# Further rows' parts in one operand, the 128 rows stored first, a later broadcast, and the last gate product in parts

## The reference, cut to what matters

```python
def hierarchical_moe(n, ...):              # 16 experts, 2 for each token
    for e in range(N_EXPERTS):
        hdn = jax.nn.silu(t @ w1[e]) * (t @ w3[e])
        out = out + gate[:, e:e + 1] * (hdn @ w2[e])

    h = h + hierarchical_moe(rms_norm(h, W['g_ffn'][l]), ...)
    gate = jax.nn.sigmoid(rms_norm(h, W['g_ple'][l]) @ W['w_ple_gate'][l])
    h = h + gate * (p[l] @ W['w_ple_proj'][l])
return rms_norm(h, W['g_final'])
```

## Time and profile before

| | |
|---|---|
| median of 3 runs | 770.13 us (769.03 to 772.84) |
| profiled execution | 769.56 us, of which the span of its instructions is 767.9 us |
| PE busy | 730.7 us, 95% |
| DVE, ACT, POOL busy | 396.6 us (52%), 318.6 us (41%), 135.2 us (18%) |
| mean granted clock of TensorE | 0.982 |
| DMA | 169.10 MB, mean 220 GB/s |

### The profile page before, as it was taken

How to read it: one execution, slowest core, us unless ns; L and a number is a source line. 1 busy time by engine, 2 the same in 40 slices (tenths; PEclk the granted TensorE clock), 3 DMA queues, 4 the chain that set the end, 5 groups by cost and what they waited for, 6 DMA issues and landing times.

```text
span 767.9 us, 11872 instructions
## 1 busy us (share of the span) xinstructions
PE 730.7 (95%) x4428; PEld 627.7 (82%) x4429; DVE 396.6 (52%) x623; ACT 318.6 (41%) x554; POOL 135.2 (18%) x168
## 2 busy tenths in 40 slices
PE   3999999999999989999999999999999999879995
PEld 2887778787888858989987987999999999738884
DVE  4987987894655466313431331343344333366663
ACT  5608659664402125314431331443444433384242
POOL 3645105060001002000000000000000000043320
PEclk9999999999999969999999999999999999999999
DMA  9909924404043258877997495699999999353202
GB/s 320 289 1 321 266 51 150 165 1 159 33 155 147 90 212 293 294 253 271 360 369 243 176 358 175 253 343 353 348 351 330 335 336 366 117 193 111 103 35 82
DMA packets 78127, 169.10 MB, mean 220 GB/s; under 512 B 7556, under 2 KB 19272, under 8 KB 78088
## 3 DMA queue, kind: packets, MB, share of 16 engines
q1 hardware_dynamic: 69968, 141.53, 52.5%
q0 software_dynamic: 4448, 14.62, 6.1%
q10 hardware_dynamic: 3672, 12.42, 4.2%
HBM read 144.50 MB, written 24.05 MB: 220 GB/s over the span
## 4 chain that ended last, share of the span: by engine, by line
PE 92%; DVE 2%; ACT 2%; DMA 1%; issue 1%; POOL 1%; ACTq 1%; POOLq 0%; DVEq 0%
PE bank L712 34%; PE bank L911 32%; PE bank L920 5%; PE bank L701 5%; PE bank L922 5%; PE bank L921 5%; PE bank L693 3%; PE bank L833 2%; PE bank L889 2%; DMA regT<-y_scratch,slots 1%; DMA y_scratch<-regN 1%; ACT ring_r L415 0%; ACTq L1087 0%; ACT regN L1067 0%; DVE regN L1337 0%
## 5 line engine op out<-in xcount | busy, mean ns | idle before, releaser
L712 PE MATMUL bank<-ring_r,regT_r 128*128 128x512 f32 x624 | 162.3, 394 | 1.7 <-DVE regT_r L1444 1.7
L712 PEld LDWEIGHTS bank<-ring_r,regT_r 128*128 128x128 f32 x624 | 116.5, 188 | 28.0 <-issue 4.5
L911 PE MATMUL bank<-regT,ring 128*128 128x128 f32 (+1 forms) x1024 | 125.4, 284 | 1.9 <-issue 0.9
L911 PEld LDWEIGHTS bank<-regT,ring 128*128 128x128 f32 x1024 | 123.3, 194 | 4.5 <-issue 4.1
L911 PE MATMUL bank<-regN,ring 128*128 128x128 f32 (+1 forms) x1024 | 123.2, 281 | 0.1
L911 PEld LDWEIGHTS bank<-regN,ring 128*128 128x128 f32 x1024 | 122.1, 191 | 1.3 <-issue 0.6
L617 POOL DMA_INDIRECT regT<-n_scratch,idsi x17 | 16.0, 940 | 323.5 <-PEq L878 209.4
L1653 DVE TENSOR_TENSOR regR<-regR,bank 128x320 f32<-128x320 f32 x32 | 15.6, 486 | 103.4 <-ACT regR L1198 103.4
L712 PE MATMUL bank<-regT_r,ring_r 128*128 128x256 f32 (+1 forms) x256 | 65.3, 344 | 2.9 <-DVE ring_r L423 2.9
L921 PE MATMUL bank<-ring_r,regR_r 128*128 128x512 f32 (+1 forms) x160 | 63.0, 394 | 0.0
L1198 ACT ACTIVATE regR<-bank 128x320 f32<-128x320 f32 x32 | 14.0, 437 | 109.5 <-PE bank L911 109.4
(11 more groups left out here) (283 smaller groups left out, 1206.5 us busy)
## 6 DMA issues: line engine op xcount, KB each, us to landing
ring<-in_w_exp_down SPq DMA_DIRECT2D x16, 2048.0 KB, 15.8
ring<-in_w_exp_gate SPq DMA_DIRECT2D x16, 2048.0 KB, 9.5
ring<-in_w_exp_up SPq DMA_DIRECT2D x16, 2048.0 KB, 16.2
ring<-in_w_in SPq DMA_DIRECT2D x4, 2048.0 KB, 10.7
y_scratch<-zeros SPq DMA_DIRECT2D x4, 1408.0 KB, 12.6
y_scratch<-regN ACTq DMA_DIRECT2D x11, 384.0 KB
h<-in_x_sample SPq DMA_DIRECT2D x8, 512.0 KB, 10.3
y_scratch<-zeros SPq DMA_DIRECT2D x4, 1024.0 KB, 11.2
```

The lines of the kernel that those rows point to most:

```text
L712: q = nc.tensor.matmul(out, a, b, start=(n == 0), stop=(n == len(passes) - 1))
L911: q = nc.tensor.matmul(bank[b][:, col:col + n], slot3(s)[:, k, f * P:(f + 1) * P], moe["xT", par][:, k, 0:n], start=(k == 0), stop=(k == K ...
```

## The change

Four edits.

1. The further rows' high and low parts lie side by side in one tile, `more_parts`, 64 columns wide. One matmul against the high weights gives both products (high by high in partitions 0 to 31 of the bank, low by high in 32 to 63); a second one, 32 columns wide, adds high by low. That is 8 matmuls for each half of the output where there were 12. The two parts of the bank must be added afterwards: DVE adds partitions 32 to 63 of bank 4 and of bank 5 to what was copied, and a new semaphore `y2_summed` tells of it. PE waits for it before it fills these banks again. `hid`'s product, its high copy and its low part are made separately for the 128 and for the further rows (two operations where one was). A clearing of 32 more partitions of bank 5 is added ahead of the first expert.
2. ACT stores the 128 rows before it copies the further rows, and stores those when `y2_summed` has come.
3. The broadcast into `gF` is issued after the first tile's high parts (after `high_n3T(0)`), no longer ahead of `take_embed(1, 0)`.
4. The last tile's gate product comes in parts of 512, 256 and 256 columns, each with its own sigmoid, multiply, add, multiplication by `gF` and sum of squares; the three sums are added on DVE, then DVE scales columns 0 to 511 and ACT columns 512 to 1023 by 1/rms, and SP stores the two halves.

The diff, cut to its core:

```diff
-            def down(out, par, lo, n, j, chunks):
+            def down(out, par, j, chunks):
...
+            def further_down(out, par, j):
+                for f in range(F4):
+                    q = nc.tensor.matmul(out[0:2 * CAP2, :], more_parts[:, f, :], down_hi[f][j], start=(f == 0), stop=(f == F4 - 1))
+                    if f < F4 - 1:
+                        for g in range(2 * f, min(2 * f + 2, F4)):
+                            nc.tensor.matmul(out[0:CAP2, :], more_hi[:, g, :], down_low(par, g, j), start=False, stop=False)
+                return q
...
                                 pe.wait_ge(ylo_drained, 2 * r)
+                                pe.wait_ge(y2_summed, r)
...
-                    down(bank[4], par, P, CAP2, 0, range(F4)).then_inc(tlo_full, 1)
-                    down(bank[5], par, P, CAP2, 1, range(F4)).then_inc(thi_full, 1)
+                    pe.wait_ge(more_done, 2 * r + 2)
+                    further_down(bank[4], par, 0).then_inc(tlo_full, 1)
+                    further_down(bank[5], par, 1).then_inc(thi_full, 1)
...
             pe.wait_ge(yhi_drained, 2 * (NE + more))
+            pe.wait_ge(y2_summed, NE + more)
...
             def hid_high_half(r, half):
+                two = slice(2 * half, 2 * half + 2)
                 act.wait_ge(hid_raw, 2 * r + half + 1)
-                nc.scalar.activation(hid_hi[:, 2 * half:2 * half + 2, :], hid[:, 2 * half:2 * half + 2, :], ACT.Copy).then_inc(hid_high, 1)
+                nc.scalar.activation(hid_hi[:, two, :], hid[:, two, :], ACT.Copy).then_inc(hid_high, 1)
+                act.wait_ge(more_raw, 2 * r + half + 1)
+                nc.scalar.activation(more_hi[:, two, :], more_hid[:, two, :], ACT.Copy).then_inc(more_high, 1)
...
-                act.wait_ge(thi_full, r + 1)
-                nc.scalar.activation(moe["y2", par][:, 512:D], bank[5][0:CAP2, :], ACT.Copy).then_inc(yhi_drained, 1)
-                act.wait_ge(yhi_drained, 2 * r + 2)
-                act.wait_ge(ylo_drained, 2 * r + 2)
+                act.wait_ge(yhi_drained, 2 * r + 1)
+                act.wait_ge(ylo_drained, 2 * r + 1)
...
+                act.wait_ge(thi_full, r + 1)
+                nc.scalar.activation(moe["y2", par][:, 512:D], bank[5][0:CAP2, :], ACT.Copy).then_inc(yhi_drained, 1)
+                act.wait_ge(yhi_drained, 2 * r + 2)
+                act.wait_ge(ylo_drained, 2 * r + 2)
+                act.wait_ge(y2_summed, r + 1)
...
-            act.dma_start(gF, g_final.partition_broadcast(P)).then_inc(gF_in, 16)
             take_embed(1, 0)
             high_n3T(0)
+            act.dma_start(gF, g_final.partition_broadcast(P)).then_inc(gF_in, 16)
...
+            last_gate(0)
+            last_sumsq(0)
+            last_gate(1)
+            last_sumsq(1)
+            last_gate(2)
+            last_sumsq(2)
+            act.wait_ge(part_scaled, 3)
+            act.wait_ge(fin_rstd, NT)
+            nc.scalar.activation(ntok[:, LAST, 512:D], ntok[:, LAST, 512:D], ACT.Copy, scale=frstd[:, LAST:NT]).then_inc(half_norm, 1)
...
+            post(V.memset(bank[5][CAP2:2 * CAP2, 2 * NE:], 0.0))
...
-                V.tensor_copy(moe["y2", par][:, 0:512], bank[4][0:CAP2, :]).then_inc(ylo_drained, 1)
+                low, high = moe["y2", par][:, 0:512], moe["y2", par][:, 512:D]
+                V.tensor_copy(low, bank[4][0:CAP2, :]).then_inc(y2_part, 1)
+                dve.wait_ge(y2_part, r + 1)
+                V.tensor_tensor(low, bank[4][CAP2:2 * CAP2, :], low, ALU.add).then_inc(ylo_drained, 1)
+                dve.wait_ge(yhi_drained, 2 * r + 2)
+                V.tensor_tensor(high, bank[5][CAP2:2 * CAP2, :], high, ALU.add).then_inc(y2_summed, 1)
...
+            for part, (name, at, n) in enumerate(last_parts):
+                dve.wait_ge(act_drained, drain_count[name])
+                here = slice(at % 512, at % 512 + n)
+                V.tensor_tensor(pgm[:, at // 512, here], pp_sb[2 * LAST + at // 512][:, here], sig[:, at // 512, here], ALU.mult).then_inc(pgm_done, 1)
+                dve.wait_ge(pgm_done, 2 * LAST + part + 1)
+                hs = h[:, LAST, at:at + n]
+                V.tensor_tensor(hs, hs, pgm[:, at // 512, here], ALU.add).then_inc(h_ready, 1)
+                dve.wait_ge(h_ready, 2 * LAST + part + 1)
+                V.tensor_tensor(ntok[:, LAST, at:at + n], hs, gF[:, at:at + n], ALU.mult).then_inc(part_scaled, 1)
```

More of the change, by code:

```diff
@@ L255, in hybrid_encoder_kernel @@
         hid_raw, hid_high = sem("hid_raw"), sem("hid_high")
+        more_raw, more_high, more_done = sem("more_raw"), sem("more_high"), sem("more_done")
+        y2_part, y2_summed = sem("y2_part"), sem("y2_summed")
         down_high_done, down_low_done = sem("down_high_done"), sem("down_low_done")
@@ L532, in _ @@
             sp.dma_start(w_pp, w_ple_proj.rearrange("(k p) n -> p k n", p=P)).then_inc(ring_in[3], 16)
-            for i in range(NT):
+            for i in range(LAST):
                 sp.wait_ge(fin_norm, i + 1)
                 sp.dma_start(token_rows(y_prompt, y_sample, i), ntok[:, i, :]).then_inc(stored, 16)
-            sp.wait_ge(stored, 16 * NT)
+            for done, value, cols in ((fin_norm, NT, slice(0, 512)), (half_norm, 1, slice(512, D))):
+                sp.wait_ge(done, value)
+                sp.dma_start(token_rows(y_prompt, y_sample, LAST)[:, cols], ntok[:, LAST, cols]).then_inc(stored, 16)
+            sp.wait_ge(stored, 16 * (NT + 1))
         @block.gpsimd
@@ L968, in one_round @@
                     for j in range(2):
-                        q = down(bank[6 + j], par, 0, P, j, (2 * half, 2 * half + 1))
+                        q = down(bank[6 + j], par, j, (2 * half, 2 * half + 1))
                         if half == 1:
@@ L1017, in _ @@
                     pe.wait_ge(yhi_drained, 2 * (NE + j))
+                    pe.wait_ge(y2_summed, NE + j)
                     over_ids(j)
@@ L1054, in _ @@
                 ple_gate(i, 0)
-                if i + 1 < NT:
+                if i < LAST:
                     turn_h(i + 1)
-                ple_gate(i, 1)
+                    ple_gate(i, 1)
+            for part in last_parts[1:]:
+                ple_gate_last(*part)
         @block.scalar
@@ L1305, in _ @@
                 take_embed(i, j)
-            for i in range(NT):
-                if i + 1 < NT:
-                    high_n3T(i + 1)
-                    ple_sumsq(i + 1)
+            for i in range(LAST):
+                high_n3T(i + 1)
+                ple_sumsq(i + 1)
                 act.wait_ge(rstd_done, 2 * NT + i + 1)
@@ L1652, in hid_half @@
                 dve.wait_ge(silu_done, 2 * r + half + 1)
-                V.tensor_tensor(hid[:, 2 * half:2 * half + 2, :], silu[:, 2 * half:2 * half + 2, :],
-                                bank[2 * half + 1][:, :].rearrange("p (f s) -> p f s", f=2)[:, :, 0:CAP], ALU.mult).then_inc(hid_raw, 1)
+                two = slice(2 * half, 2 * half + 2)
+                up = bank[2 * half + 1][:, :].rearrange("p (f s) -> p f s", f=2)
+                V.tensor_tensor(hid[:, two, :], silu[:, two, 0:P], up[:, :, 0:P], ALU.mult).then_inc(hid_raw, 1)
+                V.tensor_tensor(more_hid[:, two, :], silu[:, two, P:CAP], up[:, :, P:CAP], ALU.mult).then_inc(more_raw, 1)
                 dve.wait_ge(hid_high, 2 * r + half + 1)
-                V.tensor_tensor(hid_lo[:, 2 * half:2 * half + 2, :], hid[:, 2 * half:2 * half + 2, :],
-                                hid_hi[:, 2 * half:2 * half + 2, :].bitcast(F32), ALU.subtract).then_inc(hid_done, 1)
+                V.tensor_tensor(hid_lo[:, two, :], hid[:, two, :], hid_hi[:, two, :].bitcast(F32), ALU.subtract).then_inc(hid_done, 1)
+                dve.wait_ge(more_high, 2 * r + half + 1)
+                V.tensor_tensor(more_lo[:, two, :], more_hid[:, two, :], more_hi[:, two, :].bitcast(F32), ALU.subtract).then_inc(more_done, 1)
             def split_down(r, par):
@@ L1735, in _ @@
             split_gate_low("pg1")
-            for i in range(NT):
-                if i + 1 < NT:
-                    low_n3T(i + 1)
+            for i in range(LAST):
+                low_n3T(i + 1)
                 if i + 2 < NT:
```

48 lines of the change are left out of this document (40 added, 8 removed).

## The result

The changed kernel takes 759.63 us as the median of four runs (757.64 to 761.11), the kernel before beside it 769.89 (769.03 to 772.84). The ratio is 0.9876, with a 95% interval of 0.9844 to 0.9909: 1.2% faster. 760.3 was forecast, 757.0 to 762.8 as the range. The profiled execution has a span of 758.0 us, where the sum had 758.1. So close a hit says little of its parts: they were off in both directions.

The account below looks back on a forecast made before the run. PE's matmul chain was taken as the bound through experts and gate tiles, but not at the seam and tail. Further rows -7.4, seam -0.8, tail -1.6 gave -9.8: 770.1 to 760.3 us, range 757.0 to 762.8.

Parts of the forecast that it names:

- Further rows: Four large experts on PE: 16 matmuls each instead of 24, gain 7.4 us, bounds 7.0 to 7.5.
- The round's slack: Split of hid in every expert: 1.04 us of slack before PE needs the low part; cost on the path zero.
- The clearing: Added clearing of bank 5 before the row counts: costed at nothing, at most 0.45 us.
- The seam: Between last expert and first gate tile: +0.4 for the small store, -1.2 for the gather, together -0.8 us.
- Edit 2 may delay the seam: Seam: the small store, issued 0.87 us later behind DVE's addition, lands 0.4 us later.
- my bracket for the small store: Its landing at the seam: 0.9 us later without queueing behind the large store, 0.5 sooner if that sets it.
- -1.2 for the broadcast: Seam: without the broadcast beside it, the second gather gains 1.2 us, between 0 and 1.9.
- The tail: Behind the last matmul: split gate product, shorter operations and half stores gain 1.6 us, between 0.6 and 2.2.
- The clock at the seam: Rival: shorter PE idle time keeps the clock up, another 1.8 us gained, 758.5 us; chance 0.39.
- the seam is longer: Rival: small store takes 4.02 us from its later issue, gathers gain nothing, +0.9 instead of -0.8, 762.0 us; chance 0.05.
- the 64 columns: Rival: changing between 64 and 32 stationary columns costs, further rows gain nothing, 767.7 us; chance 0.03.
- the chain in the rounds: Rival: hid's split outgrows its 1.04 us slack and PE waits in all 16 rounds, 775.7 us; chance 0.03.

Follow-up runs that it names:

- e10: Changed kernel with the further rows' product in three passes of 32 columns and DVE's two additions replaced by copies; 768.17 us, run once.
- e8: Changed kernel with five extra reductions on DVE in every expert, ahead of the second half's low part; 766.37 us, ratio 0.9991.
- e6: e5 with the clearing of bank 5 also moved behind the row counts on DVE; 759.16 us, ratio 0.9891.
- e11: The kernel before, unchanged, run once more for a second profile; 764.30 us.
- e2: Changed kernel with the store order undone: further rows copied first, both stores issued together after the additions; 759.21 us, ratio 0.9870.
- e1: Changed kernel with store order, broadcast and tail undone, leaving the further rows' parts in one operand; 759.89 us, ratio 0.9892.
- e3: Changed kernel with the broadcast into gF issued again ahead of take_embed(1, 0); 758.31 us, ratio 0.9853.
- e12: The changed kernel again, unchanged, timed beside e9; 757.37 us, ratio 0.9876.
- e5: Changed kernel with PE waiting for the bank drains and y2_summed only ahead of the fifth embed product; 756.90 us, ratio 0.9872.
- e9: e5 with four chunks of ACT's second gate weight split moved behind the first tile's high parts and sum of squares; 755.44 us, ratio 0.9855.
- e7: Changed kernel with eight unused transposes of the identity on PE just ahead of its wait at the seam; 760.08 us, ratio 0.9899.

## Why the prediction was right, and where not

**What bounds the kernel: right.** In the experts a matmul taken away is time taken away, and nothing that was added on ACT and DVE shows (no wait of PE at a down product, small experts 20.9 as before).

**Further rows: right in kind, too small.** 4 x 8 x 0.231 = 7.4 was predicted; e10 shows 7.3 for just that. The experts gained 8.4: the other 0.9 (350.96 to 350.06 in e10) comes with the new tiles, in which all down matmuls run a little closer. The sum had no term for that.

**The round's slack: right.** The chain became 0.2 us shorter, and the slack is 1.0 by e8.

**The clearing: wrong.** It was put at nothing, because the first expert waits for ACT's copies. By the profiles (e6) the row counts come 0.97 us later and hold the first expert: 0.4 us against the kernel before, 0.6 against e11.

**The seam: wrong in its steps.** "Edit 2 may delay the seam", +0.4: it brings the first gather 1.1 us and the second addition 0.5 us sooner (e2). That end of my bracket for the small store was the true one. "-1.2 for the broadcast": the contention is there, 1.8 us of the second addition between e1 and e2, but only while the small store lands late; with edit 2 in, edit 3 brings nothing (e3). I had added up two edits that work on the same delay. "ACT is free just when PE has them": it was within a few tenths of being the bound, and it is the bound in most profiles, because its stores now wait for DVE and its weight split begins 0.8 us later (5.5 behind the last expert, also in e1 and e2, and 4.7 before). And PE's wait for `y2_summed` I cost at 0.4 of a gap that would hide it; it started PE 0.9 later and there was no gap left. The changed kernel's seams are 19.3 and 18.8, those of the kernel before 20.6 and 18.0. So -0.8 is neither shown nor refuted; what is shown is that edits 2 and 3 together take at most 0.5 off it (e1, e12), and that one profile of before was not enough to build on.

**The tail: right in kind, a little large.** 1.5 from the sigmoid on and 0.3 given back by PE, 1.2 net where 1.6 was said. Up to the end of the scaling it takes 3.92 us where 3.90 was forecast. The term that was off is the stores: 0.7 us less for half the bytes, for which no row stood. From the end of the scaling to the end it is 3.28, where 2.95 was said and the one whole store of the kernel before took 3.04.

**The sum.** Against 9.8: experts 2 to 16 1.0 more than forecast, tail 0.4 less, first expert 0.2 shorter, stages ahead of the experts 1.9 later, seam and gates 1.7 shorter, which with the 0.3 of edit 4 is 2.0 for the seam where 0.8 was said. That gives 9.9. Of the 1.9, 1.5 are there before the lists of rows, in code that is the same in both kernels, and 0.4 is the clearing. The total was right partly by luck: the experts and the seam gained more than forecast, the stages ahead of them lost what no term held, and of these the seam's part and the 1.5 are chance.

**Rivals.** The clock at the seam did go both ways (it held in e6 and fell in the changed kernel), but not for the reason I gave; whether the seam is longer depends on which profile of the kernel before is taken; the 64 columns cost nothing; the chain in the rounds held.

## What to carry to other kernels

Where PE is the bound and a product is made in several passes with few stationary columns, put the parts side by side in one operand: here 64 columns cost what 32 do, and each matmul saved was its full 0.23 us. A new wait on a sum delays whatever stands behind it, so put it before the first use of the bank that it guards; here that started PE 0.8 us sooner (e5), but shortened the seam only once ACT's queue was cut too (e9). Behind every such wait look at the engine whose queue moved. Edits that work on the same delay hide each other: undone alone, edit 3 looked worthless, and only the pair e1 and e2 showed its price. A small operation in a chain that ends in a count or a flag is not free because another wait ended last: follow what the count itself releases. Before pricing a stage by one profile, see a second of the same kernel: the steady stages repeat within 0.1 to 0.2 us, those around an idle time by 3.

## What the runs showed of the hardware

A 16 KB store issued 0.7 us behind one of 384 KB on the same queue landed 2.4 to 4.0 us after its issue (four profiles); issued 2.2 us behind it, about 1.8 us after (ten profiles). A gather of 512 KB took 6.9 us to land in the two profiles with the 512 KB broadcast issued 0 to 1.3 us behind it, and 5.2 to 5.8 in the twelve others. 24 matmuls of 512 columns took 5.33 us from the first start to the last with the stationary operand in one compact tile, and 5.42 with it strided over 160 columns; that the stride is the cause was not isolated. TensorE's granted clock fell to 0.50, its lower level of 1.2 GHz, in the first embed products of twelve of fourteen profiles, for 3.2 to 5.7 us, which made them 1.6 to 2.8 us longer; one of these is e7, where PE had worked until 0.2 us before.
